# Whole weight jobs in every second round of the dense attention loops

## What is computed

```python
def diff_attention(qc, kc, vc, bias_cols, lam, subln_g, lam_init):
    ...
    def one_block(args):
        j, qj = args
        ...
        logits = jnp.einsum('bqhmc,bkhmc->bhmqk', qj, kf) * scale + bias[None, :, None]
        p = jax.nn.softmax(logits, axis=-1)
        a = p[:, :, 0] - lam * p[:, :, 1]
        return jnp.einsum('bhqk,bkhe->bqhe', a, vf)
    o = lax.map(one_block, (jnp.arange(nq), qb))
    ...

y_a = fourier_mix(a_in) @ w_br_a[l]
gates = jax.nn.sigmoid(u @ w_gate[l] + b_gate[l]).reshape(Bsz, S, N_BRANCHES, D)
merged = gates[:, :, 0] * y_a + gates[:, :, 1] * y_b + gates[:, :, 2] * y_c
```

## Time and profile before

| what | value |
|---|---|
| median of 3 runs | 3668.08 us (3663.72 to 3670.44) |
| the profiled execution | 3667.71 us, its span 3665.9 us |
| PE busy | 3475.9 us, 95% of the span |
| DVE busy | 1592.1 us, 43% |
| ACT busy | 1348.8 us, 37% |
| POOL busy | 1482.1 us, 40% |
| share of the chain that ended last | PE 88%, DVE 7%, ACT 2%, issue 2% |

### The profile page before, as it was taken

The page is one execution under the profiler, slowest core; times in us unless marked ns, Lnnn a source line. Parts: engine busy times, 40 slices in busy tenths (PEclk is TensorE's granted clock), DMA queues, the critical chain, the costliest instruction groups (busy, mean ns, idle before and its releaser), DMA issues.

```text
span 3665.9 us, 49960 instructions
## 1 busy us (share of the span) xinstructions
PE 3475.9 (95%) x16490; PEld 2859.5 (78%) x16490; DVE 1592.1 (43%) x2321; ACT 1348.8 (37%) x2354; POOL 1482.1 (40%) x1124
## 2 busy tenths in 40 slices
PE   8999999899999999999999999999988897789997
PEld 6888888688888888878877888887768886568886
DVE  3223623854322432244357442324876666243224
ACT  4233324544322432242255342324562233233322
POOL 3444532254444454454222644444220034134443
PEclk9999999999999999999999999999999998989998
DMA  3222321232222322232121322223110012113222
GB/s 109 97 97 97 124 75 63 69 101 98 96 94 97 104 98 97 97 122 99 64 69 60 115 97 97 97 93 103 59 63 12 7 52 86 40 60 101 95 95 91
DMA packets 87626, 310.69 MB, mean 85 GB/s; under 512 B 9889, under 2 KB 11937, under 8 KB 87384
## 3 DMA queue, kind: packets, MB, share of 16 engines
q1 hardware_dynamic: 82512, 297.97, 24.3%
q10 hardware_dynamic: 5000, 11.22, 1.1%
HBM read 306.95 MB, written 2.20 MB: 84 GB/s over the span
## 4 chain that ended last, share of the span: by engine, by line
PE 88%; DVE 7%; ACT 2%; issue 2%; DMA 0%; ACTq 0%; POOL 0%; DVEq 0%; POOLq 0%; SPq 0%
PE ps L439 25%; PE ps L441 25%; PE ps L440 25%; PE ps L863 1%; PE ps L872 1%; PE ps L606 1%; PE ps L866 1%; PE ps L460 1%; PE ps L462 1%; PE ps L461 1%; PE ps L621 1%; PE ps L933 1%; PE ps L562 0%; PE ps L772 0%; DVE x L1797 0%
## 5 line engine op out<-in xcount | busy, mean ns | idle before, releaser
L404 POOL TENSOR_TENSOR w_lo<-raw,w_hi 128x512 fp32r<-128x512 f32 x1120 | 1481.9, 1328 | 2154.3 <-ACT w_hi L965 2150.6
L439 PE MATMUL ps<-u_hi,w_hi 128*128 128x512 f32 (+1 forms) x2990 | 1175.7, 393 | 37.9 <-POOL w_lo L404 10.1
L965 ACT ACTIVATE w_hi<-raw 128x512 fp32r<-128x512 f32 x1120 | 692.2, 629 | 1289.4 <-PE ps L441 1225.5
L441 PE MATMUL ps<-u_lo,w_hi 128*128 128x512 f32 (+1 forms) x2990 | 1159.6, 388 | 0.0
L440 PE MATMUL ps<-u_hi,w_lo 128*128 128x512 f32 (+1 forms) x2990 | 1159.1, 388 | 0.0
L439 PEld LDWEIGHTS ps<-u_hi,w_hi 128*128 128x128 f32 x2990 | 568.9, 190 | 169.0 <-issue 32.1
L440 PEld LDWEIGHTS ps<-u_hi,w_lo 128*128 128x128 f32 x2990 | 568.9, 190 | 114.8 <-issue 4.1
L441 PEld LDWEIGHTS ps<-u_lo,w_hi 128*128 128x128 f32 x2990 | 567.8, 190 | 114.3
L1516 DVE TENSOR_TENSOR T<-ps,rs 128x512 f32<-128x512 f32 x268 | 185.2, 691 | 740.0 <-PE ps L441 737.4
L439 PE MATMUL ps<-m_hi,w_hi 128*128 128x512 f32 x1216 | 477.1, 392 | 10.1 <-DVE m_lo L1520 6.9
L440 PE MATMUL ps<-m_hi,w_lo 128*128 128x512 f32 x1216 | 474.2, 390 | 0.0
(11 more groups left out here) (431 smaller groups left out, 2875.8 us busy)
## 6 DMA issues: line engine op xcount, KB each, us to landing
raw<-jobs SPq DMA_DIRECT2D x560, 512.0 KB, 3.3
tab<-vec_dram ACTq DMA_DIRECT2D x8, 448.0 KB, 5.3
x<-x_in SPq DMA_DIRECT2D x4, 512.0 KB, 6.5
out<-x SPq DMA_DIRECT2D x8, 256.0 KB, 2.1
tab<-dft_in ACTq DMA_DIRECT2D x2, 901.0 KB, 4.7
pt<-share_dram ACTq DMA_DIRECT2D x4, 384.0 KB, 4.9
tab<-chunk_in ACTq DMA_DIRECT2D x1, 1024.0 KB, 4.9
tab<-mem_in ACTq DMA_DIRECT2D x4, 256.0 KB, 3.0
```

The costliest lines, as they stand in the source:

```text
L404: pool.tensor_tensor(w_lo[:, s, w], raw[:, s, w], w_hi[:, s, w].bitcast(F32), ALU.subtract).then_inc(lo_done[s], 1)
L439: pe.matmul(ps[bank][:, 0:n], w_hi[:, s, w], hi[:, k, 0:n], start=k == ks[0], stop=False)
L441: last = pe.matmul(ps[bank][:, 0:n], w_hi[:, s, w], lo[:, k, 0:n], start=False, stop=k == ks[-1])
L965: act.activation(w_hi[:, s, half_of(half)], raw[:, s, half_of(half)], ACT.Copy).then_inc(hi_done[s], 1)
```

## The change

In an even round PE now issues no weight job at all. In an odd round it issues both halves of one job, between `transposes(u)` and `values(u)`. The job that had its halves in rounds 2j and 2j+1 is now whole in round 2j+1. Number, kind and size of all instructions stay the same. The wait for the input tiles (`ready`) that stood in rounds 0 and 1 is now in round 1 for both halves.

```diff
@@ -632,7 +632,9 @@
                     transposes(u)
                     if u == 0:
                         scores(2)
-                    half_job(u // 2 % 2, u % 2, m_hi, m_lo, ready=(m_ready, c.now("m")) if u < 2 else None)
+                    if u % 2:
+                        for half in range(2):
+                            half_job(u // 2 % 2, half, m_hi, m_lo, ready=(m_ready, c.now("m")) if u == 1 else None)
                     values(u)
```

## The result

The changed kernel takes 3722.53 us (median; 3720.80 to 3725.43) against 3665.91 us (3663.72 to 3670.44) for the kernel before. The ratio is 1.0153 with a 95% interval of 1.0141 to 1.0165, so the change makes the kernel 56.6 us slower. The profiled execution has a span of 3721.1 us, 55.2 us more than the one before.

What follows compares the result with a forecast made beforehand. PE was taken as the bound, DVE not far behind. The profiled 3667.7 us plus 39 for both dense loops and 8.5 for clock falls gave 3715.2, about 3715.5 at the median; range 3703 to 3724.

Steps and rivals of the forecast that it cites:

- clock term: Falls of PE's clock behind long idle stretches in both loops: 5 falls, 8.5 us; bounds 0 and 13.6.
- The walk through a middle pair: Rounds 2 to 13: PE waits 0.93 us for ACT's copy, 1.60 for DVE; pair takes 13.03 us instead of 10.58.
- the row of the dilated stage: Same ACT copy in an earlier stage: PE goes on 0.65 us after it starts, taken as the copy's release time.
- Rounds 14 and 15: End of each dense loop, without scores and logits: 8.5 us from transposes to values where it was 7.6, +0.9 us.
- The mix rounds: DVE's mix_group ahead of the gate product in passes 6, 8 and 10 delays PE's transposes: 1.1 us a loop.
- Round 1: Start of each loop: transposes still wait for DVE, then a whole job follows instead of half: +2.8 us.
- That term: Added time of both dense loops without clock falls: 19.5 us a loop, 39 us.
- the four long stretches of a loop: PE idle in round 1 (3.4 us) and the mix pairs (2.9, twice 3.6): 2.5 clock falls a loop.
- the lower anchor of the interpolation: Clock taken never to fall behind 2.19 us of PE idle time, since it stayed at 1.00 there once.
- The clock did not fall in every pair: Rival: clock falls in all 16 pairs of the dense loops, 27 us in place of 8.5, 3734 us; chance 0.07.
- That only the copy is paid: Rival: a pair costs only PE's 0.93 us wait for ACT's copy, 15 us, giving 3683 us; chance 0.04.
- the long job gives DVE a lead: Rival: DVE runs ahead during the 5.6 us whole job, removing five waits a loop, 3657 us; chance 0.03.

Runs made afterwards that it cites:

- the filled kernel: Changed kernel plus 8 thrown-away matmuls (128x512) of PE ahead of the transposes of rounds 1, 7, 9 and 11: 3707.35 us.
- The mirror: Changed kernel with the whole job in every even round and none in the odd ones: 3689.39 us, a fourth execution of 11502 us left out.
- the 2 + 6 kernel: Kernel before with each job cut into two k in the even round and six in the odd one, in place of four and four: 3691.37 us.
- its repetition: The changed kernel run once more, unaltered, for its trace alone: 3724.07 us, one execution.
- the two pairs of repeated traces: Changed kernel and kernel before, each traced once more without alteration: 3724.07 us and 3668.11 us, one execution each.
- the single steps: Kernel before with DVE's five mix_group instructions spread singly over the odd passes 5, 7, 9, 11 and 13: 3664.54 us.
- 5 + 3: Kernel before with each job cut so that the even round gets five parts and the odd round three, in place of four and four: 3667.64 us.

## Why the prediction was right, and where it was off

The forecast was 3715.5 us in a range of 3703 to 3724, and 3722.5 was measured, near the upper end. As a difference the miss is a little larger: 47.4 us of slowdown were forecast from the 3668.1 of the kernel before, and 56.6 were measured against its 3665.9. The range held partly by luck. Its upper edge had been drawn for errors of 0.2 us in the walk, which did not come, and they left room for a clock term that came out above its own upper bound. And three things that the forecast said of the profile did not hold: the dense loops take 113.5 and 114.2 us and not 108 to 112, the clock falls four times in each and not two or three times, and about 4 us came outside the loops.

**The walk through a middle pair** held within 0.03 us: 13.06 measured, 13.03 forecast. Values start 1.42 us behind the transposes where I had 1.34, so the copy's release takes a little longer than the row of the dilated stage let me think, and the values after a wait take 1.08 us in place of 0.98. Neither matters for the pair, since PE waits for DVE next: transposes(u+1) start 6.10 us behind the scores, against 6.04, and the wait in front of them is only the shorter for it, 1.42 in place of 1.60. Transposes and job take 5.98 against 6.01.

**Rounds 14 and 15** had 8.5 us from transposes to values in the forecast and have 8.50 (767.63 to 776.13). **The mix rounds** were to stand still for 2.9 and twice 3.6 us and did for 2.6 and twice 3.3. **Round 1** stood still for 3.36 against 3.4. Without the clock a loop is 18.9 us longer, against 19.5 forecast: the first loop's 25.3 less four falls of 1.6, and the second loop's 25.9 less three of 1.6 and the long one of 2.2. That term was 39 us and is about 38.

**The term that was mis-sized is the clock: 8.5 us forecast, about 17 measured.** I gave the four long stretches of a loop chances between 0.4 and 0.75, on a straight line from "never at 2.19 us" to "always at 4.06". In the trace all eight brought a fall. Two more came behind the loops, at the very 2.19 us that I had taken as safe, and one fall of the second loop lasted twice as long. In sum these are seven falls of 1.6 us and one of 2.2 in the loops, 13.4 us, and two of 1.6 behind them. The price of one fall (1.7 us) was right: 1.6 in the pairs, 1.6 from the filled kernel. The failed step is thus the lower anchor of the interpolation. One loop in which 2.19 us had left the clock up showed that it can stay up, and I read it as showing that it does. Even my upper bound for this term, all eight stretches, was 13.6, since it left out the two behind the loops.

**The rivals.** The clock did not fall in every pair. Idle times of 0.76 and 1.42 us next to each other, with only values and scores between them, were never followed by a fall in any trace of this case. The rule of the Trainium skill ("TensorE: Matmul & The Clock Gate", section "A second HAM failure mode: psum-queue depth-cycling"), by which repeated short idle times make the clock swing, does not show at these lengths; what fell in and behind the dense loops fell at single stretches of over 2 us (elsewhere in these traces it did fall without one, see the last section). That only the copy is paid is refuted by the waits for L1694. That the long job gives DVE a lead is refuted by the same rows: DVE starts on the scores' heels at 681.00 in the pair shown, and had been idle before. The mirror shows how it would have to be: the cover must stand in the round whose DVE pass is the long one.

## What to carry to other kernels

Work that fills the waits of a pipeline is worth its place, not its amount: the same 24 matmuls cost no more than their own time when each round has 12, and 38 us on top when every second round has none, because each round has latencies of its own (here a copy of 0.9 us and a DVE pass of 2.5 us) that cover in the next round cannot pay for. Before moving such work, walk once through a round with the starts and releases of the trace; it gave the pair within 0.03 us. And for every idle stretch of PE that a change makes longer than about 2 us, add the price of a fall of the clock, here 1.6 us. In this case the chance was about one half just above 2 us (16 of 28) and near one from 2.6 (26 of 30), but these are few kinds of stretches, met again and again.

## What the runs showed of the hardware

In the dense loops the clock's falls follow the idle stretches of PE, but not by a sharp limit. In and just behind the dense loops of the thirteen traces of this case, none of the idle stretches of 1.2 to 2.0 us brought a fall (0 of 32), 16 of 28 of those of 2.16 to 2.42 us did, and 26 of 30 of those of 2.6 to 3.4 us. (These counts are worked out from the start times of the matmuls and the granted clock over time in each trace.) The length alone does not decide: three of the four misses are stretches of 2.94 to 2.97 us in the 2 + 6 kernel, where only one of four brought a fall, while all four of 2.6 us in the changed kernel and its repetition did. In the two pairs of repeated traces the outcomes at these stretches were the same, yet between kernels the identical stretch of 2.19 us behind the loops went either way. What else decides is open.

A long idle stretch is not needed either. In the kernel before, the clock falls four times between 525 and 577 us, in the dilated stage ahead of the first loop, and PE has no idle stretch over 0.69 us there. What stands ahead of these falls are small matmuls. PE around one of them, and windows of 3 us on both sides of the fall:

```profile
538.73 1.00 PE L590 MATMUL ps<-pt,T 128*128 128x64 f32 x8
539.66 2.24 PE L562 MATMUL ps<-pt 64*128 64x128 f32 x8
541.83 0.56 PE L439 MATMUL ps<-u_hi,w_hi 128*128 128x512 f32 x1
```

```profile
539.00:542.00 3.00, 3.00 (x16) 2.72 (x16) 0.76 (x2) 0.56 (x1) 1.28 (x1) 1.00 0.00 0
542.20:545.20 3.00, 3.00 (x9) 2.33 (x8) 1.80 (x3) 0.63 (x1) 0.00 (x0) 0.50 0.50 162
```

That the small matmuls are the cause is not shown: the same instructions run in every kernel of this case, and the clock falls four times there in four traces, three times in five, once in one and not at all in three. The first loop starts accordingly (its `scores(1)`): at 654.4 to 655.2 us with four falls, 652.3 to 653.2 with three, 650.4 with one and 648.8 to 649.5 with none, some 1.2 to 1.4 us for each fall. The changed kernel had four falls in one trace and three in the other. The time between the loops (1142.1 to 1148.1 us) and behind them (1657.0 to 1663.3 us) varies as much, though the experiments change next to nothing there. So a difference of a few us between whole executions, as in the single steps or in 5 + 3, says little in this kernel; the length of the two loops in the trace, which repeats within 0.1 us where the falls are the same, says more.

Work thrown away can pay: 64 matmuls in idle stretches made the two loops of the changed kernel 13.6 us shorter, since they kept PE's clock at 2.4 GHz for the job behind them.
